# Piece 22 of each expert loaded as 112 and twice 8 partitions

## The chip, the cores and the metric

One core of a Trainium2 chip. The metric is the device time of one execution in microseconds (us), median over runs. A core has five engines (TensorE or PE, VectorE or DVE, ScalarE or ACT, GpSimd or POOL, SyncE or SP) and 16 transfer engines, which move data between the chip's main memory and its on-chip memory of 128 partitions. SP issues nearly all transfers here, in one queue; a transfer of 128 partitions is spread over all 16 transfer engines, eight partition rows each.

## What is computed

A two-layer decoder on 256 tokens of width 1024, in float32: latent attention, a dense feed-forward block, sliding-window attention, and then a mixture of experts, a final norm at the end. The experts are what matters here:

```python
gates = ...                                     # top 2 of 8 experts per token, softmax over the two
hg = jnp.einsum('sd,edf->sef', xs, w_gate)      # e = 8 experts, d = 1024, f = 3584
hu = jnp.einsum('sd,edf->sef', xs, w_up)
hh = jax.nn.silu(hg) * hu * gs[..., None].astype(xs.dtype)
return jnp.einsum('sef,efd->sd', hh, w_down)
```

Each expert has three matrices of 1024 x 3584 float32 values, 44 MB together, and all eight experts are read once: 352 MB.

## The kernel before, in words

The dense part takes the first 400 us. Then come eight items, one per expert (more only if an expert has over 96 tokens). The experts are ordered at run time, so that those with up to 64 tokens ("narrow") and those with more ("wide") come in a fixed pattern; a narrow item is less work for TensorE, while every item has the same weights.

An expert's weights come in 24 pieces of 128 partitions x 3584 values (14336 bytes per partition, 1792 KB): pieces 0 to 7 of the gate matrix, 8 to 15 of the up matrix, 16 to 23 of the down matrix (the list `pieces`, `NP` = 24). A ring of eight places in on-chip memory holds them. SP runs `load_item`: for each piece it waits in `room_for` until TensorE has read what lies in that place, and issues the transfer. Its semaphore is one of eight (`landing`), each raised by 16 for a landed piece. Piece 23 is loaded as two halves by columns (L708 and L709 in the profile), the second on the semaphore `tail_landed`, so that TensorE can begin with its first half.

TensorE takes an item in this order (`pe_item`): the products with the eight gate pieces (`products`, L1569), among them the scatter of the item before (L1587); those with the eight up pieces (L1569); the first 14 rows of the down product (`down`, L1611 and L1612 in a narrow item, L1544 to L1548 in a wide one); the gather of the next item's tokens (L1535); and the other 14 down rows. A down row is 1024 columns wide, so that 3.5 rows lie in a piece: row r begins at column 1024 r of the down pieces, and piece 16 + n at column 3584 n. A row in a narrow item is two passes of a pair of matmuls (L1611 and L1612, side by side). `down` waits for a piece with `piece_here` before the first row that reaches into it: for piece 22 before row 21, for the second half of piece 23 before row 26. The wait is on the whole count, so a piece is there when the last of its transfer engines has finished.

Instructions are themselves brought in by transfers, in the queue named "instruction" (q8), in packets of 16 KB.

Of the kernel before, what the change touches and what calls it, by code (L numbers as in the profile page):

```python
# [37 lines left out]
P = 128  # L38
# [90 lines left out]
class Semaphores:  # L129
    def __init__(self, sem):  # L130
# [124 lines left out]
        self.ahead_loaded_a = sem("ahead_loaded_a")  # L255
        self.ahead_loaded_c = sem("ahead_loaded_c")
        self.tail_landed = sem("tail_landed")
        self.gu_read = sem("gu_read")
        self.gate_mm = sem("gate_mm")
        self.sg_ready = sem("sg_ready")  # L260
# [21 lines left out]
def build(nc, x, positions, w_in, g_q, g_kv, w_uq, w_ukv, w_o, kv_g, kv_w, kv_b, swa_w_q, swa_b_q,  # L282
          swa_sinks, swa_w_o, swa_b_o, rel_bias, g_attn, g_ffn, f_gate, f_up, f_down, w_router,
          e_gate, e_up, e_down, g_final, consts, out):
    with ExitStack() as ctx:
# [12 lines left out]
        s = Semaphores(lambda name: ctx.enter_context(nc.semaphore(name)))  # L298
# [253 lines left out]
        pieces = [(kind, 0, k) for kind in "gu" for k in range(KD)]  # L552
        pieces += [("d", half, part) for half in range(2) for part in range(TILES * D // PIECE)]
        NP = len(pieces)
        DOWN0 = 2 * KD
        assert NP % LAPS == 0 and KD == LAPS
        ppos = {p_: m for m, p_ in enumerate(pieces)}
        whole = ring[:].rearrange("p a n -> p (a n)")

        def turn_of(m, first):  # L560

            return m if first and m < 2 * KD - OUTSIDE else m - OUTSIDE

        def place(m, first):

            return PIECE * ((FIRST_AT + turn_of(m, first)) % LAPS)

        def landing(m, first):

            return s.piece_landed[turn_of(m, first) % LAPS]  # L570
# [5 lines left out]
        def piece_here(eng, i, m, first):  # L576

            if first and m in AHEAD_A:
                eng.wait_ge(s.ahead_loaded_a, 16 * OUTSIDE)
            else:  # L580
                eng.wait_ge(landing(m, first), i * (16 * NP // LAPS) + 16 * (turn_of(m, first) // LAPS + 1))

        def piece(m, first):
            if first and m in AHEAD_A:
                return AHEAD_A[m]
            return whole[:, place(m, first):place(m, first) + PIECE]

        def down_row(r):

            c0 = (place(DOWN0, False) + D * r) % (LAPS * PIECE)  # L590
            return whole[:, c0:c0 + D]

        def down_pieces(r):

            return range(DOWN0 + D * r // PIECE, DOWN0 + (D * r + D - 1) // PIECE + 1)

        def last_down_row(m):

            return (PIECE * (m + 1 - DOWN0) - 1) // D

        def in_tail(r):

            return D * r + D > PIECE * (NP - DOWN0) - PIECE // 2

# [45 lines left out]
        def _(sp):  # L650
# [11 lines left out]
            def piece_of_expert(m, expert):  # L662
                kind, half, part = pieces[m]
                if kind == "d":
                    return ed[:, expert, half, part * PIECE:(part + 1) * PIECE]
                return (eg if kind == "g" else eu)[:, expert, part, :]

            def room_for(i, m, first):

                if m < LAPS:  # L670
                    if not first:
                        sp.wait_ge(s.down_mm, i * (2 * TILES) + (last_down_row(m + 2 * LAPS) + 2 - 2 * TILES))
                        return
                    for sl in dense_under(m):
                        if sl >= 5:
                            sp.wait_ge(*used_up(NU - 1))
                        else:
                            sp.wait_ge(*stream[earlier_fill(DENSE, sl)][4:6])
                    return
                under = m - LAPS  # L680
                if first and m >= DOWN0:
                    in_ring = [p_ for p_ in range(NP) if p_ not in AHEAD_A]
                    under = in_ring[in_ring.index(m) - LAPS]
                kind, _, k = pieces[under]
                if k < KD - 1:
                    sp.wait_ge(s.gu_read, i * (2 * KD - 2) + ((KD - 1) * (kind == "u") + k + 1))
                else:
                    sp.wait_ge(s.gate_mm if kind == "g" else s.up_mm, i * (2 * THIRDS) + 2 * THIRDS)

            def load_item(i, expert, first):  # L690
                for m in range(NP):
                    if first and m == 5:
                        sp.wait_ge(s.spT_mm, AH)
                        for ma, room in AHEAD_A.items():
                            sp.dma_start(room, piece_of_expert(ma, expert)).then_inc(s.ahead_loaded_a, 16)
                    if first and m == LAPS:
                        sp.wait_ge(s.swo_mm, 4)
                        sp.wait_ge(s.router_mm, 2)
                        for ma, room in AHEAD_C.items():
                            sp.dma_start(room, piece_of_expert(ma, expert)).then_inc(s.ahead_loaded_c, 16)  # L700
                    if first and (m in AHEAD_A or m in AHEAD_C):
                        continue
                    room_for(i, m, first)
                    if m < NP - 1:
                        sp.dma_start(piece(m, first), piece_of_expert(m, expert)).then_inc(landing(m, first), 16)
                    else:
                        src, mid = piece_of_expert(m, expert), PIECE // 2
                        sp.dma_start(piece(m, first)[:, 0:mid], src[:, 0:mid]).then_inc(landing(m, first), 16)  # L708
                        sp.dma_start(piece(m, first)[:, mid:PIECE], src[:, mid:PIECE]).then_inc(s.tail_landed, 16)  # L709

            load_item(0, 0, True)
            sp.wait_ge(s.counts_ready, 1)
            sp.wait_ge(s.order_ready, 1)
            with sp.Fori(1, NE) as i:
                load_item(i, sp.value_load(order[0:1, bass.ds(i, 1)], min_val=0, max_val=NE - 1), False)

            items = sp.value_load(n_items[0:1, 0:1], min_val=NE, max_val=ITEMS_MAX)
            for sweep in range(1, SWEEPS):
                with sp.If(items > sweep * NE):
                    with sp.Fori(0, NE) as e:  # L720
                        load_item(e + sweep * NE, sp.value_load(order[0:1, bass.ds(e, 1)], min_val=0, max_val=NE - 1), False)
                with sp.Else():
                    sp.nop()
# [356 lines left out]
        def _(pe):  # L1080
# [460 lines left out]
            def wide_step(bank, slots, left, right, first, last):  # L1541
                thirds = [slots[:, 32 * j:32 * j + 32] for j in range(3)]
                for j in range(3):
                    pe.matmul(ps[32 * j:32 * j + 32, bank, :], thirds[j], left, start=first, stop=last)  # L1544
                pe.matmul(ps[SLOTS:P, bank, :], thirds[2], right, start=first, stop=last)  # L1545
                for j, cols in ((0, 0), (1, 0), (0, LASTQ), (1, LASTQ)):
                    q = 32 * j + cols // 4
                    mm = pe.matmul(ps[q:q + 32, bank + 1, 0:LASTQ], thirds[j], right[:, cols:cols + LASTQ], start=first, stop=last)  # L1548
                return mm
# [46 lines left out]
            def down(i, half, j, narrow, first_item):  # L1596
                r = half * TILES + j
                for m in down_pieces(r):
                    if r == 0 or m not in down_pieces(r - 1):
                        piece_here(pe, i, m, first_item)  # L1600
                if in_tail(r) and not in_tail(r - 1):
                    pe.wait_ge(s.tail_landed, i * 16 + 16)
                if r == 0:
                    pe.wait_ge(s.sgt_ready, i + 2)
                if j == 0:
                    pe.wait_ge(s.hhT_ready, i * 2 + (half + 1))
                w = down_row(r)
                first, last = r == 0, r == 2 * TILES - 1
                if narrow:
                    lhs = hhT[:, half, j, 0:NARROW]  # L1610
                    pe.matmul(ps[0:NARROW, DOWN_BANK, :], lhs, w[:, 0:512], start=first, stop=last)  # L1611
                    mm = pe.matmul(ps[64:64 + NARROW, DOWN_BANK + 1, :], lhs, w[:, 512:1024], start=first, stop=last)  # L1612
                else:
                    mm = wide_step(DOWN_BANK, hhT[:, half, j, :], w[:, 0:512], w[:, 512:1024], first, last)
                mm.then_inc(s.down_mm, 1)
# [555 lines left out]
```

## Time and profile before

| | |
|---|---|
| median of 3 runs | 1222.96 us (1222.02 to 1223.16) |
| profiled execution, its own time | 1221.85 us |
| its span, first to last instruction | 1220.0 us |
| mean granted TensorE clock | 0.989 of full speed |
| TensorE matmul busy | 1163.6 us, 95% of the span |
| moved by transfers | 413.44 MB, 339 GB/s over the span |
| expert phase | from about 403 to 1208 us |

TensorE's busy share and the transfer engines' share are both near full in the expert phase. A share of 1.00 of the transfer engines means that all 16 are at work; it can read a little above 1, as packets of one engine overlap slightly. Items of the expert phase are numbered 0 to 7.

### The profile page before, as it was taken

How to read it: one execution, taken by the hardware profiler on the slowest of the kernel's cores; microseconds unless marked ns; L12 is line 12 of the kernel's file. 1: busy time of each engine (PE TensorE's matmuls, PEld its weight loads, DVE VectorE, ACT ScalarE, POOL GpSimd, SP SyncE). 2: the span in 40 equal slices, each digit the busy share in tenths (PEclk: the TensorE clock that was granted, in tenths of full speed). 3: DMA queues.
4: the chain of work that ended last, by engine and by line, in shares of the span. 5: the costliest groups of instructions: out<-in, count | busy, mean ns of one | idle time of the engine just before them, and what ended most of it. 6: DMA issues, size and time to landing. Idle time of an engine off the chain costs nothing.

```text
span 1220.0 us, 21797 instructions
## 1 busy us (share of the span) xinstructions
PE 1163.6 (95%) x9461; PEld 584.5 (48%) x9462; DVE 338.9 (28%) x727; ACT 212.9 (17%) x399; POOL 40.0 (3%) x69
## 2 busy tenths in 40 slices
PE   7999999999999999799899999999989989998997
PEld 5878777778765534233233433333343333333323
DVE  3666566666372302002002010110201101020112
ACT  2454333333263100000010000001010010101001
POOL 2130000000200010000000000000000000000000
PEclk9999999999999999899899999999999999999999
DMA  9614645237534999999999999999999999999994
GB/s 338 243 69 161 229 162 190 87 138 256 220 122 181 375 417 426 415 427 425 425 425 426 414 414 426 425 426 425 426 426 425 426 425 426 425 424 424 421 425 195
DMA packets 56044, 413.44 MB, mean 339 GB/s; under 512 B 4702, under 2 KB 10076, under 8 KB 32140
## 3 DMA queue, kind: packets, MB, share of 16 engines
q1 hardware_dynamic: 54464, 410.40, 82.1%
q8 instruction: 82, 1.34, 0.4%
q0 software_dynamic: 944, 1.29, 0.3%
q10 hardware_dynamic: 540, 0.29, 0.1%
q14 instruction: 14, 0.11, 0.0%
HBM read 410.91 MB, written 1.05 MB: 338 GB/s over the span
## 4 chain that ended last, share of the span: by engine, by line
PE 85%; DMA 4%; DVE 4%; issue 4%; ACT 2%; ACTq 0%; POOL 0%; POOLq 0%; DVEq 0%; SPq 0%
PE ps L1569 36%; PE ps L1611 7%; PE ps L1544 6%; PE ps L1256 4%; PE ps L1252 4%; PE ps L1253 4%; PE ps L1548 3%; PE ps L1587 3%; PE ps L1535 2%; PE ps L1428 2%; DMA ring<-in_moe_w_gate 2%; DMA ring<-in_moe_w_down 2%; PE ps L1379 2%; PE ps L1115 2%; ACT w_hi L912 1%
## 5 line engine op out<-in xcount | busy, mean ns | idle before, releaser
L1569 PE MATMUL ps<-ring,arena 128*32 128x448 f32 x4800 | 465.9, 547 | 23.9 <-issue 21.7
L1569 PEld LDWEIGHTS ps<-ring,arena 128*32 128x32 f32 x4800 | 155.6, 111 | 327.0 <-issue 324.5
L1611 PE MATMUL ps<-ring,arena 128*64 128x512 f32 x280 | 122.9, 594 | 8.2 <-DVE arena L2111 5.1
L1612 PE MATMUL ps<-ring,arena 128*64 128x512 f32 x280 | 122.9, 594 | 0.0
L2106 DVE TENSOR_TENSOR arena<-arena,ps 128x448 f32<-128x448 f32 x38 | 22.3, 605 | 285.1 <-PE ps L1569 284.7
L1544 PE MATMUL ps<-ring,arena 128*32 128x512 f32 x504 | 87.0, 593 | 2.4 <-DVE arena L2111 2.4
L1852 DVE TENSOR_TENSOR w_lo<-ring,w_hi 128x2048 fp32r<-128x2048 f32 x31 | 71.1, 2292 | 57.1 <-ACT w_hi L912 55.1
L1545 PE MATMUL ps<-ring,arena 128*32 128x512 f32 x168 | 85.9, 593 | 0.0
L1611 PEld LDWEIGHTS ps<-ring,arena 128*64 128x64 f32 x280 | 37.2, 137 | 87.1 <-issue 71.6
L912 ACT CAST w_hi<-ring 128x2048 fp32r<-128x2048 f32 x31 | 59.1, 1909 | 112.9 <-PE ps L1256 112.9
L2088 DVE TENSOR_TENSOR h<-h,ps 128x512 f32<-128x512 f32 x36 | 24.8, 688 | 186.3 <-PE ps L1587 186.3
L1024 ACT ACTIVATE arena<-ps 128x448 f32<-128x448 f32 x38 | 20.6, 543 | 258.0 <-PE ps L1569 257.2
L1252 PE MATMUL ps<-w_hi,xT_hi 128*128 128x512 f32 (+1 forms) x176 | 64.9, 376 | 0.0
L1253 PE MATMUL ps<-w_hi,xT_lo 128*128 128x512 f32 (+1 forms) x176 | 63.9, 370 | 0.0
L1031 ACT ACTIVATE arena<-ps,vecT 128x96 f32<-128x96 f32 x36 | 9.3, 341 | 299.5 <-PE ps L1535 299.5
L1548 PE MATMUL ps<-ring,arena 128*32 128x256 f32 x672 | 51.6, 379 | 0.0
L1548 PEld LDWEIGHTS ps<-ring,arena 128*32 128x32 f32 x672 | 21.8, 110 | 50.3 <-issue 50.3
L1256 PE MATMUL ps<-w_lo,xT_hi 128*128 128x512 f32 (+1 forms) x176 | 41.4, 379 | 0.0
L1612 PEld LDWEIGHTS ps<-ring,arena 128*64 128x64 f32 x280 | 37.2, 137 | 0.0
L1587 PE MATMUL ps<-arena 96*128 96x512 f32 x72 | 35.6, 618 | 0.8 <-ACT arena L1055 0.8
L1252 PE MATMUL ps<-w_hi,fhhT_hi 128*128 128x512 f32 x88 | 34.8, 395 | 1.4 <-DVE h L1921 1.4
L1535 PEld LDWEIGHTS ps<-arena,xn 128*128 128x128 f32 x288 | 32.9, 192 | 6.2 <-issue 5.9
(306 smaller groups left out, 1157.9 us busy)
## 6 DMA issues: line engine op xcount, KB each, us to landing
ring<-in_moe_w_gate SPq DMA_DIRECT2D x64, 1792.0 KB, 19.2
ring<-in_moe_w_up SPq DMA_DIRECT2D x61, 1792.0 KB, 16.5
ring<-in_moe_w_down SPq DMA_DIRECT2D x56, 1792.0 KB, 21.1
ring<-in_moe_w_down SPq DMA_DIRECT2D x16, 896.0 KB, 22.0
ring<-in_ffn_w_gate SPq DMA_DIRECT2D x5, 2048.0 KB, 7.8
ring<-in_ffn_w_up SPq DMA_DIRECT2D x5, 2048.0 KB, 7.8
ring<-in_ffn_w_down SPq DMA_DIRECT2D x5, 2048.0 KB, 7.9
ring<-in_mla_w_o SPq DMA_DIRECT2D x2, 2048.0 KB, 24.6
```

The costliest lines, as they stand in the source:

```text
L912: act.copy(hi, w).then_inc(s.whi_ready, 1)
L1252: pe.matmul(out, lhs[0][:, k, c], rhs_hi[:, k, :], start=(first and k == 0), stop=False)
L1253: pe.matmul(out, lhs[1][:, k, c], rhs_hi[:, k, :], start=False, stop=False)
L1256: mm = pe.matmul(out, lhs[0][:, k, c], rhs_lo[:, k, :], start=False, stop=(last and k == nk - 1))
L1544: pe.matmul(ps[32 * j:32 * j + 32, bank, :], thirds[j], left, start=first, stop=last)
L1545: pe.matmul(ps[SLOTS:P, bank, :], thirds[2], right, start=first, stop=last)
L1548: mm = pe.matmul(ps[q:q + 32, bank + 1, 0:LASTQ], thirds[j], right[:, cols:cols + LASTQ], start=first, stop=last)
L1569: mm = pe.matmul(ps[Q * q:Q * q + Q, bank_of(a, j), 0:CH], lhs, w[:, c0:c0 + CH], start=first, stop=last)
L1587: pe.matmul(ps[:, SCATTER_BANK[j], :], sgt[0:SLOTS, t, :], ysb[0:SLOTS, half * 512:(half + 1) * 512], start=True, stop=True).then_inc(s.sc ...
L1611: pe.matmul(ps[0:NARROW, DOWN_BANK, :], lhs, w[:, 0:512], start=first, stop=last)
L1612: mm = pe.matmul(ps[64:64 + NARROW, DOWN_BANK + 1, :], lhs, w[:, 512:1024], start=first, stop=last)
L1852: dve.tensor_tensor(lo, w, hi.bitcast(F32), ALU.subtract).then_inc(s.wlo_ready, 1)
```

## The change

Piece 22 (`CORNERED = NP - 2`) of each expert is no longer one transfer of 128 partitions. SP issues two of eight partitions, 112 to 119 and 120 to 127, on a semaphore of their own, and then one of partitions 0 to 111 on the piece's usual semaphore. The large one is spread over all 16 transfer engines as seven rows each; each of the small ones goes as one row to each of eight engines, so that eight engines get nine rows of the piece, and eight get seven. The bytes and their places are the same. TensorE waits for the new semaphore too, right after the piece's own, before row 21. SP waits for room as before, once, ahead of the three.

```diff
+        self.corner_landed = sem("corner_landed")
...
+        CORNERED, CORNERS = NP - 2, ((P - 16, P - 8), (P - 8, P))
...
                     room_for(i, m, first)
-                    if m < NP - 1:
+                    if m == CORNERED:
+                        room, src = piece(m, first), piece_of_expert(m, expert)
+                        for p0, p1 in CORNERS:
+                            sp.dma_start(room[p0:p1, :], src[p0:p1, :]).then_inc(s.corner_landed, 16)
+                        whole_rows = CORNERS[0][0]
+                        sp.dma_start(room[0:whole_rows, :], src[0:whole_rows, :]).then_inc(landing(m, first), 16)
+                    elif m < NP - 1:
                         sp.dma_start(piece(m, first), piece_of_expert(m, expert)).then_inc(landing(m, first), 16)
...
                         piece_here(pe, i, m, first_item)
+                        if m == CORNERED:
+                            pe.wait_ge(s.corner_landed, i * (16 * len(CORNERS)) + 16 * len(CORNERS))
```

## Rows read from the trace of the kernel before

**Rows 1.** The page: share and rate of the transfer engines in 40 equal slices.
```profile
DMA  9614645237534999999999999999999999999994
GB/s 338 243 69 161 229 162 190 87 138 256 220 122 181 375 417 426 415 427 425 425 425 426 414 414 426 425 426 425 426 426 425 426 425 426 425 424 424 421 425 195
```

**Rows 2.** Stretches of 100 us: busy times, then clock, transfer share, GB/s.
```profile
800.00:900.00 100.00, 99.22 (x1057) 37.44 (x1053) 12.64 (x21) 4.66 (x11) 0.00 (x0) 1.00 1.01 425
900.00:1000.00 100.00, 93.02 (x794) 33.57 (x786) 11.45 (x20) 6.98 (x15) 0.00 (x0) 0.98 1.01 425
```

**Rows 3.** TensorE's waits, 499 to 1200 us: total, times, longest (us).
```profile
PE ps L1569 <- issue: 21.7, 5, 9.1
...
PE ps L1611 <- DMA ring<-in_moe_w_down: 3.0, 2, 1.5
...
PE ps L1569 <- DMA ring<-in_moe_w_gate: 2.1, 1, 2.1
```

**Rows 4.** Transfers in the chain that ended last: start, length (us).
```profile
972.95 27.81 DMA ring<-in_moe_w_gate
...
1165.00 23.44 DMA ring<-in_moe_w_down
```

**Rows 5.** SP's timeline: issue of the gate pieces of items 6 and 7.
```profile
972.95 26.41 SPq L705 DMA_DIRECT2D ring<-in_moe_w_gate  x8
...
1084.42 35.05 SPq L705 DMA_DIRECT2D ring<-in_moe_w_gate  x8
```

**Rows 6.** TensorE's timeline in the down rows of item 7: start, length (us).
```profile
1177.83 0.64 PE L1611 MATMUL ps<-ring,arena 128*64 128x512 f32 x1 [1.00 <-DVE arena L2111]
...
1183.46 0.59 PE L1611 MATMUL ps<-ring,arena 128*64 128x512 f32 x1
...
1184.14 0.64 PE L1611 MATMUL ps<-ring,arena 128*64 128x512 f32 x1
...
1186.34 0.59 PE L1611 MATMUL ps<-ring,arena 128*64 128x512 f32 x1
...
1188.48 0.64 PE L1611 MATMUL ps<-ring,arena 128*64 128x512 f32 x1 [1.54 <-DMA ring<-in_moe_w_down]
...
1195.81 0.64 PE L1611 MATMUL ps<-ring,arena 128*64 128x512 f32 x1
```

**Rows 7.** End of the weight stream: stretch, length, clock, transfer share, GB/s.
```profile
1194.00:1196.00 2.00, 1.00 1.03 434
...
1198.00:1199.00 1.00, 1.00 0.51 203
...
1202.00:1203.00 1.00, 1.00 0.52 215
...
1205.00:1206.00 1.00, 1.00 0.00 0
```

**Rows 8.** Queues from 794 to 898.6 us: packets, MB, share of 16 engines.
```profile
q1 hardware_dynamic: 3622, 44.37, 100.2%
q8 instruction: 9, 0.15, 0.6%
```

**Rows 9.** The same columns as in rows 7, 695 to 696 us.
```profile
695.00:696.00 1.00, 1.00 0.64 272
```

**Rows 10.** TensorE's timeline at the start of item 6.
```profile
1000.99 1.33 PE L1569 MATMUL ps<-ring,arena 128*32 128x448 f32 x12 [2.14 <-DMA ring<-in_moe_w_gate]
```

**Rows 11.** SP's timeline: issue of the two halves of piece 23, item 7.
```profile
1177.02 0.33 SPq L708 DMA_DIRECT2D ring<-in_moe_w_down  x1
1177.54 0.33 SPq L709 DMA_DIRECT2D ring<-in_moe_w_down  x1
```

**Rows 12.** The lines L708 and then L709: their eight issues to landing.
```profile
DMA to landing us min/median/max: 13.3/20.9/26.4
...
DMA to landing us min/median/max: 15.0/22.5/28.0
```

**Rows 13.** Transfers to few partitions: times, KB each, us to landing.
```profile
posk_i<-in_positions POOLq DMA_DIRECT2D x4, 8.0 KB, 5.4
```

## Prediction

> **What bounds the kernel now.** I read the page's slices first, then the stretches, TensorE's waits, the chain of waits, the timelines, and last the end of the weight stream and the queues. The reader is to see three things.
>
> First, in the expert phase two resources are nearly full at once. From the page's slices the transfer engines (DMA engines) are full from about 430 us to almost the end [rows 1], and in a stretch of 100 us they show a share of 1.01 at 425 GB/s while TensorE is busy for 99.22 us; in another it is busy for only 93.02 us at the same transfer rate [rows 2]. So the weights come at one steady pace, and TensorE is sometimes ahead of them and sometimes not.
>
> Second, where TensorE really waits for a transfer. After 499 us its waits are 21.7 us without a releaser, in five places at the start of an item, 2.1 us for a gate piece, 3.0 us for down pieces [rows 3]. The chain of waits goes through two transfers: one from 972.95 to 1000.76 us and one from 1165.00 to 1188.44 us [rows 4]. The first is gate piece 0 of item 6, the last but one of eight: SP issued that item's gate pieces from 972.95 us, those of item 7 from 1084.42 [rows 5]. The second is found by counting down rows: a row is two pairs of matmuls 0.43 us apart, row 0 begins at 1177.83, and the gap of 1186.34 to 1188.48 lies before row 10 [rows 6]. Row 10 is the first that reaches into piece 19 (columns from 10752). Between these two landings lie 24 + 19 = 43 pieces in 1188.4 - 1000.8 = 187.6 us: 4.36 us for one, 104.7 us for the 24 of an item. From 1000 us the pace of the weights sets the end; before, TensorE mostly does.
>
> Third, whose pace that is. A piece is 128 rows of 14336 bytes, eight for each of 16 engines; at 425/16 = 26.6 GB/s a row takes 0.54 us. But the engines do not finish together: at the end of the stream the share falls from 1.03 to 0.51 at 1198 us, stays near 0.5 until 1203 and is zero from 1205 [rows 7]. With nothing left to issue, a share of one half means that eight engines have finished and eight have about 6.5 us to go. A landing counts only when the last engine is done, so the late eight set the pace, and the early eight lead them. The instruction queue shows where such a lag can come from: nine packets of 16 KB in the stretch of one item, which go to single engines and not to all [rows 8]. The lead is also trimmed on the way: at 695 us the share falls to 0.64 for a microsecond, since the early ones had nothing queued [rows 9]. Eight packets per item and eight late engines fit: 6.5 us over the last five to seven items is 0.9 to 1.3 us per item, more than 16384 bytes at 26.6 GB/s (0.6 us), but of that size.
>
> **The change part by part.** Removed: one transfer of 128 rows per item. Added: one of 112 rows, seven per engine, and two of eight rows, one row on each of eight engines. Those eight get nine rows of piece 22, the other eight get seven; bytes are the same. All eight items do it.
>
> Engine time, if a row costs what it costs now: +0.54 us per item on eight engines, -0.54 us on the other eight. If the seven go to the late eight, the landing of piece 0 of item 6 comes 6 x 0.54 = 3.2 us sooner, that of piece 19 in item 7, before that item's own piece 22, 7 x 0.54 = 3.8 us, and the tail of item 7 4.3 us sooner. The engines with nine must not become the last. At the end they had about 6.5 us in hand; relative to the others they lose 7 x 1.08 = 7.6 us by piece 19. Taken alone this puts them 1.1 us behind and the gain at 2.7 us. But they also ran dry at 695 [rows 9] and, being later now, would not: that gives back one or two microseconds. So 2.7 to 3.8 us; I take 3.7, since at a share of 0.64 each early engine loses 0.36 x 16/8 = 0.7 us in that microsecond alone, and pays the start of a new transfer besides.
>
> What TensorE can take of it: the wait of 2.14 us at item 6 [rows 10], and 0.25 us at 1184.14 and 1.71 us at 1188.48, each a start-to-start time less the usual 0.43 [rows 6]: together 4.1 us, besides 1.5 us for a down piece before 1000 us [rows 3]. The smaller of 4.1 and 3.7 counts: 3.7 us. The profiled execution took 1221.85 us (span 1220.0 and 1.85 around it), 1.1 less than the median of the runs; the sum gives 1218.15 for it, and 1219.3 for the median. The tail does not undo it. It lands at 1177.5 + 28.0 = 1205.5 us [rows 11, 12]; row 26 of the down product, which needs it, begins near 1206.2 (row 14 at 1195.81 [rows 6], then 0.86 us a row), and it moves with the others. Further ahead little is to be had: of TensorE's waits after 499 us only three ended with a transfer, those 1.5 us, the 2.14 and the 1.54 [rows 3].
>
> Issue: SP issues two more transfers per item. One is 0.33 us, and the next follows 0.52 us later [rows 11], so some 1.0 us per item. Queued behind them are the rest of piece 22, the two halves of piece 23, and the next item's pieces. They land typically 20.9 to 22.5 us after issue [rows 12], so the engines have some four pieces queued; the delay is hidden as long as that holds. If the queue were empty it would cost 1.0 us per item. The shortest landing of the first half of piece 23 is 13.3 us [rows 12], still three pieces. TensorE gets one more wait per item, before row 21; its weight load sits idle about 0.3 us before each pass, and a passed wait is taken as nothing (upper bound 8 x 0.1 us).
>
> What the trace does not show is the price of a row in the two small transfers. Eight rows go at the same time into eight neighbouring partitions, 112 to 119 and then 120 to 127, while other engines write their own. Lower bound: 0.54 us a row, as now. Upper bound: the eight share what one engine moves now, 8 x 0.54 = 4.3 us for each transfer, 7.5 us more per item than at the lower bound. The nearest rows are loads of 32 and fewer partitions of 8 KB and less, 5.4 us to landing [rows 13], which excludes neither. I take the lower bound, because every row of the stream so far runs at 26.6 GB/s whatever the phase of the other engines, but both ends stay for the range.
>
> The Trainium skill speaks against this part. "SBUF — State Buffer", section "Door 1: The DMA port swizzle", says that a transfer's rate depends on how many of 16 ports its partitions reach, four neighbouring partitions (and those 32 above) sharing one; a 16-partition load was measured there at 104 GB/s. By that page 112 to 119 are two ports, and the estimate from it is 2.1 us for each small transfer instead of 0.54. This trace has no large transfer on few partitions, so no run here shows it.
>
> "DMA: Bandwidth & Descriptors", section "Why a DMA increments its semaphore by 16 and not by 1", says that a transfer of eight partitions from SP uses the lowest-numbered eight engines. The trace carries no engine numbers, so it does not say whether these are the early ones.
>
> **The rivals.**
> (a) Forecast: the early eight get nine, rows keep their price. 1222.96 - 3.7 = 1219.3 us.
> (b) The rows of the small transfers slow each other. Place: piece 22 of each item, on the engines with nine. Price: four rows in turn instead of side by side, 2 x (4 x 0.54 - 0.54) = 3.2 us per item. The engines with nine now need about 104.7 - 1.2 + 0.5 + 3.2 = 107.2 us per item against 104.7: 2.5 us x 8 = 20 us later, 1243 us (at the upper bound, 7.5 us per item, some 40 to 50 us more than now); more than 1243 if the engines that write these partitions anyway are held up as well. It decides from 0.5 us per item on: there it eats the whole gain, and above it the kernel is slower. For it: all these rows are issued at once into neighbouring partitions. Against: the early eight's lead, and no such slowing in this trace. The page on SBUF above is this rule.
> (c) The late eight get nine. Nothing in the trace names them. +0.54 x 7 = 3.8 us at piece 19: 1226.8 us.
> (d) No effect that can be measured: a small extra price of 0.2 to 0.5 us per item, or the late group differs from one execution to the next, so that the two halves cancel. 1222 us.
>
> **How the numbers follow.** (a) 0.47, (b) 0.30, (c) 0.10, (d) 0.13. A difference of 0.2% (2.45 us) is about what can be told from no change. Of (a) I give 0.04 to a gain below that; of (b) 0.02 to a price so small that it is in the band. Faster 0.44, same 0.18, slower 0.38. The prediction is (a), 1219.3 us, in its own range 1218.6 to 1221 us. The range over the cases goes up to 1244 us, the value of (b) just inside, and leaves out the worse part of (b), where both groups are held up or the upper bound holds: 0.13 above it, 0.02 below.
>
> **What would show it.** In the profile after: the fall of the share at the end of the stream should go from 1.0 to 0 within some 2 us instead of 6.5; the gate wait of 2.14 us at item 6 should be gone and that before row 10 smaller; the stream's end should come near 1201 us. Under (b) the rate over a stretch of 100 us drops below 420 GB/s, TensorE waits for transfers in most items, and the small transfers take longer to land than their neighbours. Under (c) the half-share stretch at the end grows to 10 us or more. The prediction is wrong if the small rows cost over 1 us each, if the late engines are those with nine, or if SP's extra issues meet an empty queue.

## The result, and the profile after

The median of four runs is 1316.3 us (1313.33 to 1319.92) against 1222.81 us of four runs before: a ratio of 1.0761, 95% interval 1.0746 to 1.0776. The change makes the kernel 93.5 us slower. The profiled execution took 1318.39 us, its span is 1316.6 us.

The page first: the rate and share of the transfer engines in 40 slices, then the queue of the weights and the issues of the down pieces (times, KB each, median us to landing).

```profile
DMA  9516444348258999999999999999999999999991
GB/s 343 200 61 255 162 160 160 129 163 309 77 203 352 412 348 424 427 336 424 427 363 356 426 427 263 427 426 350 314 423 427 278 384 410 404 310 411 426 308 60
...
q1 hardware_dynamic: 54592, 410.40, 82.3%
...
ring<-in_moe_w_down SPq DMA_DIRECT2D x48, 1792.0 KB, 27.6
```

Beside [rows 1] the second line says nearly all. The share is full in the same part of the span, but the rate is no longer one flat 425: it falls to 260 to 360 GB/s once or twice per item and comes back to 427 between. So the engines are not short of work there; what they do takes longer, and only for a while.

TensorE's waits from 480 to 1310 us (total, times, longest); L1621 and L1577 are the lines L1611 and L1569 of before, L1552 is L1544.

```profile
PE ps L1621 <- DMA ring<-in_moe_w_down: 51.0, 23, 6.1
PE ps L1577 <- issue: 24.7, 5, 9.1
PE ps L1577 <- DMA ring<-in_moe_w_up: 18.1, 18, 1.2
PE ps L1552 <- DMA ring<-in_moe_w_down: 4.9, 2, 4.5
```

The three rows with a transfer stand for 43 waits and 74 us; the three such waits of before were worth 5.1 us [rows 3]. The waits without a releaser have hardly moved (24.7 us, 21.7 before). Up pieces make TensorE wait too, so the delay is not over with piece 22.

The same in stretches of 100 us, 500 to 1300 (columns as in rows 7 of before):

```profile
500.00:600.00 100.00, 0.94 1.01 396
600.00:700.00 100.00, 0.98 1.01 386
700.00:800.00 100.00, 0.98 1.01 411
800.00:900.00 100.00, 0.95 1.01 384
900.00:1000.00 100.00, 0.97 1.01 363
1000.00:1100.00 100.00, 0.93 1.00 363
1100.00:1200.00 100.00, 0.99 1.00 376
1200.00:1300.00 100.00, 0.96 0.83 321
```

Together they moved 300 MB in 800 us. At 425 GB/s that takes 706 us: 94 us less, about the whole loss.

Where in an item it lies: SP's timeline at piece 22 of item 2, and the stretches behind it.

```profile
675.51 0.81 SPq L709 DMA_DIRECT2D ring<-in_moe_w_down  x2
676.49 0.32 SPq L711 DMA_DIRECT2D ring<-in_moe_w_down  x1
```

```profile
680.00:684.00 4.00, 1.00 1.13 326
684.00:688.00 4.00, 1.00 0.96 186
688.00:692.00 4.00, 1.00 1.01 219
692.00:696.00 4.00, 1.00 0.93 177
696.00:700.00 4.00, 1.00 1.02 233
700.00:704.00 4.00, 1.00 1.03 336
704.00:708.00 4.00, 1.00 1.01 427
```

From 684 to 700 us all 16 engines are busy and move 204 GB/s, half of the usual. That is 3.3 MB, nearly two pieces, where the changed piece alone has 1.8 MB. Pieces next to it are drawn in. The trace's records of single rows say it too. In these 16 us every row of 14336 bytes took 0.74 to 1.38 us, where the usual one takes 0.54, and there are 164 of them, more than the 128 of piece 22. Every half row of piece 23 took 0.36 to 0.77 us, where 0.27 is usual.

TensorE has 1189.8 us of matmul time against 1163.6, with a mean granted clock of 0.973 against 0.989: some matmuls behind a wait run at a lower clock. That this costs nothing is a reading, not a measurement: the transfer engines are full all the while, and the weights' pace sets the time.

### The profile page after: what moved, and what is told of

Read it like the earlier page. It is cut to its first block, busy times and chain, and to the rows that moved or that the text cites. A ratio compares the mean times of both kernels' runs of the same rounds, so it can differ in the third digit from the quotient of the medians.

```text
span 1316.6 us, 21849 instructions
## 1 busy us (share of the span) xinstructions
PE 1189.8 (90%) x9461; PEld 587.1 (45%) x9462; DVE 338.8 (26%) x727; ACT 213.0 (16%) x399; POOL 40.0 (3%) x69
## 4 chain that ended last, share of the span: by engine, by line
PE 65%; DMA 26%; issue 3%; DVE 3%; ACT 2%; ACTq 0%; SPq 0%; POOL 0%; POOLq 0%; DVEq 0%
PE ps L1577 27%; DMA ring<-in_moe_w_down 12%; DMA ring<-in_moe_w_gate 9%; DMA ring<-in_moe_w_up 4%; PE ps L1552 4%; PE ps L1264 4%; PE ps L1260 4%; PE ps L1261 4%; PE ps L1621 2%; PE ps L1595 2%; PE ps L1436 2%; PE ps L1556 2%; PE ps L1387 2%; PE ps L1123 2%; PE ps L1543 1%
## 5 line engine op out<-in xcount | busy, mean ns | idle before, releaser
L1577 PE MATMUL ps<-ring,arena 128*32 128x448 f32 x4800 | 471.1, 549 | 44.2 <-issue 24.7
L1577 PEld LDWEIGHTS ps<-ring,arena 128*32 128x32 f32 x4800 | 155.2, 111 | 353.2 <-issue 317.5
L1621 PE MATMUL ps<-ring,arena 128*64 128x512 f32 x280 | 140.3, 652 | 53.2 <-DMA ring<-in_moe_w_down 51.0
L1622 PE MATMUL ps<-ring,arena 128*64 128x512 f32 x280 | 140.4, 652 | 0.0
L1621 PEld LDWEIGHTS ps<-ring,arena 128*64 128x64 f32 x280 | 39.0, 149 | 147.8 <-issue 88.1
L1552 PE MATMUL ps<-ring,arena 128*32 128x512 f32 x504 | 88.5, 601 | 7.3 <-DMA ring<-in_moe_w_down 4.9
L1553 PE MATMUL ps<-ring,arena 128*32 128x512 f32 x168 | 87.3, 602 | 0.0
L2098 DVE TENSOR_TENSOR h<-h,ps 128x512 f32<-128x512 f32 x36 | 24.7, 687 | 189.7 <-PE ps L1595 189.7
L2132 DVE TENSOR_TENSOR arena<-ps,vecT 128x384 f32<-128x384 f32 x8 | 4.5, 557 | 140.0 <-PE ps L1543 140.0
L1622 PEld LDWEIGHTS ps<-ring,arena 128*64 128x64 f32 x280 | 39.0, 149 | 0.0
```

Of the source, the lines that this page charges most:

```text
L1577: mm = pe.matmul(ps[Q * q:Q * q + Q, bank_of(a, j), 0:CH], lhs, w[:, c0:c0 + CH], start=first, stop=last)
```

## The experiments

Three theories. A: any partition range other than all 128 makes several transfer engines write at once through the same entrance (the way into memory that a few partitions share, the prediction's port), the large 112-row transfer as much as the small ones. B: only the two small transfers do so, and the 112 rows keep their price. C: the number of transfers, issues and waits costs.

### First four: the parts of the change alone

Each stands in place of the three transfers of the change (`room` is the place in the ring, `src` the piece). One run of each and one of before (1222.27 us), on one chip; four runs of the change spread over 6.6 us, so differences of a few us between these are not to be read. The cuts of the code show the transfers alone. TensorE waits for `corner_landed` as in the change, but not in "112 alone", which never raises it.

**112 and 16.** The two small transfers made one.

```diff
+    sp.dma_start(room[112:128, :], src[112:128, :]).then_inc(s.corner_landed, 16)
+    sp.dma_start(room[0:112, :], src[0:112, :]).then_inc(landing(m, first), 16)
```

> Piece 22 of each item as one transfer of 16 partitions (112 to 127) and one of 112; every engine has eight rows, and no transfer of eight partitions is left. Theory A (the 112-partition transfer spreads its rows so that engines meet at the same partitions' entrance, and all of them slow down): most of the 93 us stay, 1290 to 1340 us. Theory B (the two transfers of eight partitions are what costs): nearly all of it goes, below 1245 us. Theory C (the nine rows on the wrong eight engines, or SP's extra issues): 1223 to 1227 us.

Measured: 1304.06 us, +81.8. So of the 93.5 us some 12 go with having two small transfers instead of one of 16 rows.

**112 alone.** Rows 112 to 127 of piece 22 are not loaded at all.

```diff
+    sp.dma_start(room[0:112, :], src[0:112, :]).then_inc(landing(m, first), 16)
```

> Only partitions 0 to 111 of piece 22 are loaded (rows 112 to 127 of it keep what an earlier piece left there, so the output is another one); seven rows per engine. Theory A: still 50 us or more above 1223. Theory B and theory C: 1216 to 1222 us, since there is less to load.

Measured: 1298.97 us, +76.7, with less to load. In the stretches behind item 2's piece 22:

```profile
684.00:688.00 4.00, 1.00 0.93 189
688.00:692.00 4.00, 1.00 1.05 224
692.00:696.00 4.00, 1.00 0.96 211
696.00:700.00 4.00, 1.00 0.98 397
```

The half rate is there with no small transfer in the kernel, only for 12 us instead of 16. This excludes B as the main cause: the 112-row transfer does it alone. (With rows left out the output is another one; the time is what counts here.)

**64 and 64.**

```diff
+    sp.dma_start(room[0:64, :], src[0:64, :]).then_inc(s.corner_landed, 16)
+    sp.dma_start(room[64:128, :], src[64:128, :]).then_inc(landing(m, first), 16)
```

> Piece 22 as two transfers of 64 partitions; four rows of each per engine. Theory A: a half of the partitions is a half of the entrances, so each row costs up to twice: 4 us or more per item, 1250 to 1300 us. Theory B and theory C: within 3 us of 1223.

Measured: 1329.32 us, +107.1, more than the change. From 900 to 1000 us the weights' queue (packets, MB, share of 16 engines) shows, of this kernel:

```profile
q1 hardware_dynamic: 2980, 35.98, 100.2%
```

and of before in the same stretch:

```profile
q1 hardware_dynamic: 3473, 42.41, 100.2%
```

The engines are as full and move 15% less.

**The small ones alone.** Partitions 112 to 119 and 120 to 127 are loaded as in the change; rows 0 to 111 of piece 22 are not loaded.

```diff
+    sp.dma_start(room[112:120, :], src[112:120, :]).then_inc(s.corner_landed, 16)
+    sp.dma_start(room[120:128, :], src[120:128, :]).then_inc(landing(m, first), 16)
```

> Only partitions 112 to 127 of piece 22 are loaded, as the two transfers of eight (the other 112 rows are left out, so the output is another one). Theory A in its strict form (the 112 rows are the cause): below 1223 us. Theory B: the 93 us stay less the 3.7 us per item of the rows left out: 1280 us or more. If rows in a small transfer cost up to four times a usual one, 3.2 us per item more on eight engines, the two nearly cancel: 1215 to 1225 us.

Measured: 1223.31 us, +1.0. The time alone says little here, since leaving out 112 rows saves 3.8 us of transfer per item, of which TensorE could have taken only some 4 us in all. The rate says more (500 to 1100 us):

```profile
500.00:600.00 100.00, 0.98 1.01 412
600.00:700.00 100.00, 1.00 1.01 412
700.00:800.00 100.00, 0.98 1.00 404
800.00:900.00 100.00, 1.00 1.01 415
900.00:1000.00 100.00, 0.98 1.01 414
1000.00:1100.00 100.00, 1.00 1.01 415
```

412 GB/s on average with full engines: 3% short of 425, about 3 us per item. The prediction gave rival (b) 3.2 us of lost time on eight engines and 2.5 us in the pace of an item. The pace is near that, but here the 3 us are a mean over all sixteen engines, twice (b)'s engine time. The records of single rows show whose it is. After 430 us, 496 rows of 14336 bytes took over 0.7 us, 127 in the kernel before; the small transfers have only 128 rows in all. So rows of the full pieces are slowed too. Half rows of piece 23 over 0.38 us are 442 of 2048, 5 before.

### Theory C: two transfers of all 128 partitions

**Halves by columns.**

```diff
+    sp.dma_start(room[:, 0:mid], src[:, 0:mid]).then_inc(s.corner_landed, 16)
+    sp.dma_start(room[:, mid:PIECE], src[:, mid:PIECE]).then_inc(landing(m, first), 16)
```

> Piece 22 as two transfers of all 128 partitions, half the columns each, with a semaphore and a wait of its own, as in the change. Theory A (partition ranges other than the full 128 are the cause): no change, within 2 us of 1223. Theory C (one more transfer, wait or issue by SP costs): over 1225 us.

Measured: 1223.63 us (10 runs) against 1223.24 (16 runs), ratio 1.000, 0.999 to 1.001. One more transfer, issue, semaphore and wait per item cost nothing that can be measured. C is out as a cause of this size.

### The same extra rows, in other partitions

Before, plus three extra loads per item in items 1 to 7 (with pieces 4, 12 and 20), of eight partitions by 8192 bytes, into space that nothing reads; TensorE waits for each together with its piece. The bytes and the count are equal; the partitions differ: every fourth of 0 to 28, every fourth of 64 to 92, or 112 to 119. The rows of the piece that are read differ with them, since each load takes the rows of its own partitions.

```diff
+    if not first and m in (4, 12, 20):
+        sp.dma_start(early_row[0:29:4, 0:2048], piece_of_expert(m, expert)[0:29:4, 0:2048]).then_inc(s.extra_landed, 16)
```

**0, 4, ..., 28.**

> The kernel before, with three extra loads of eight partitions x 8192 bytes in each of items 1 to 7 (24.6 KB per engine, 0.9 us at the usual rate, to unused space): partitions 0, 4, ..., 28. If the eight engines that a transfer of eight partitions uses are the early ones, and each meets nobody at its partition: within 1.5 us of 1223. If they are the late ones: 0.9 x 7 = 6 us more, 1229 us.

**64, 68, ..., 92.**

> The same three extra loads into partitions 64, 68, ..., 92, which in a load of 128 partitions other engines write. If two engines then meet at each entrance, the late ones lose up to what is loaded extra, 0.9 us per item: 1226 to 1232 us, between the spread and the adjacent one. If only neighbours in one transfer matter: as the spread one.

**112 to 119.**

> The same three extra loads into partitions 112 to 119, all next to each other. If four neighbouring partitions share an entrance, a row takes four times as long: 3.7 us per item on eight engines, 2.4 beyond the lead that they gain, and the engines that write there anyway are held up too: 1235 to 1255 us. If neighbours don't matter: as the spread one.

Measured: 1227.91 us (ratio 1.0034, 1.0022 to 1.0046), 1239.54 us (1.0127, 1.0110 to 1.0144) and 1250.18 us (1.0214, 1.0197 to 1.0231): +4.7, +16.3 and +26.9 us. What the eight engines have more to do is 3 x 8192 bytes per item, 0.92 us at 26.6 GB/s, 6.5 us over seven items. The first costs less than that. The other two cost 12 and 22 us on top, for as many bytes in as many rows. So which partitions a transfer covers sets the price. That it is the writing into them and not the reading of their rows is not separated here; the rule below speaks for the writing. Nor is it mainly the extra rows that take longer. By the trace's records of single rows, their medians are 0.31, 0.32 and 0.32 us in the three runs, and 0.31 us is usual for 8192 bytes. But of the rows of 14336 bytes, which belong to the full pieces, 148, 514 and 700 took over 0.7 us (after 430 us). The weights' queue from 900 to 1000 us, of the first of these kernels:

```profile
q1 hardware_dynamic: 3497, 42.37, 100.1%
```

of the second:

```profile
q1 hardware_dynamic: 3383, 41.78, 100.3%
```

of the third:

```profile
q1 hardware_dynamic: 3345, 41.48, 100.0%
```

The Trainium skill, "SBUF — State Buffer", section "Door 1: The DMA port swizzle", gives the rule: partitions 0, 4, ..., 28 and 64, 68, ..., 92 are eight different entrances each, 112 to 119 two. "DMA: Bandwidth & Descriptors", section "The descriptor swizzle", adds whose they are: in a transfer of 128 partitions, partitions 0 to 63 are written by the lower eight engines and 64 to 127 by the upper eight, each to one entrance. If the eight rows go to the eight lower engines in order, these write at their own entrances in the first run, at those of the other eight in the second, and crowd two of the others' in the third. The order of the three times agrees. Which row goes to which engine no trace here shows.

### Is 96 and 32 better, and who are the late ones?

**96 and 32.** In the form of the first experiments, with partitions 96 to 127 and then 0 to 95.

> Piece 22 of each expert is loaded as 32 partitions (96 to 127) and 96 partitions (0 to 95). Theory A (any range of partitions other than the full 128 makes engines meet at the same partitions, so that their rows take twice as long and pieces behind are drawn in): much slower, 1290 to 1340 us, like 112 and 16 (1304) and 64 and 64 (1329). Theory B (only small transfers on neighbouring partitions cost): 32 partitions are four times the 8 of one corner, so the loss per row would be smaller: below 1240 us. If 96, a multiple of 16 and of 32, is spread without meetings, the time is near 1225 us, and theory A would hold for 112 and 64 alone.

Measured: 1320.13 us (one run), against 1223.51 before on its chip. The loss that A foresees is there for each of the splits 64, 96 and 112.

The run with extra rows in 0, 4, ..., 28 told one more thing, at the end of the stream:

```profile
1206.00:1207.00 1.00, 1.00 0.53 208
1207.00:1208.00 1.00, 1.00 0.50 208
1208.00:1209.00 1.00, 1.00 0.31 129
1209.00:1210.00 1.00, 1.00 0.14 57
1210.00:1211.00 1.00, 1.00 0.12 50
1211.00:1212.00 1.00, 1.00 0.12 50
```

A share of 0.12 is two of 16. Two engines now end last, some 3 us behind the next ones. This looked as if the late eight of before were two of the eight with extra rows and six of the other half. To find the two, the same loads with fewer partitions:

**0, 4, 8, 12.**

> Before plus, in items 1 to 7, three extra loads of 4 partitions by 8192 bytes (partitions 0, 4, 8, 12, written to space that nothing reads), so that only the four lowest-numbered engines have more to do, 0.92 us per item each. If the two engines that ended last in the run with eight of them (+4.7 us) are among these four, the loss stays at 4 to 5 us and two of 16 engines are the last at the end of the stream (share 0.12); if none is, no measurable change, 1223 us, and the share at the end stays at one half until 5 us after the first fall. If one is, the loss is the same and the share at the very end is 0.06.

**0, 4, ..., 20.**

> As the run with four partitions, with six (partitions 0, 4, 8, 12, 16, 20), so that the six lowest-numbered engines have 0.92 us more per item. If the two last engines are numbers 4 and 5, this is 4 to 5 us slower than before and the run with four is not; if they are 6 and 7, neither is; if they are among the first four, both are.

Measured against 1223.51 us: 1222.57 us (ratio 0.9989, 0.9980 to 0.9999) with four, so no loss; 1227.28 us (1.0026, 1.0016 to 1.0036) with six. The difference between them is the rows in 16 and 20. The end of the stream with six:

```profile
1205.00:1206.00 1.00, 1.00 0.36 151
1206.00:1207.00 1.00, 1.00 0.12 50
1207.00:1208.00 1.00, 1.00 0.07 29
```

First two engines, then one. If a transfer of four or six partitions goes to the four or six lowest-numbered engines, as the Trainium skill's "DMA: Bandwidth & Descriptors", section "Why a DMA increments its semaphore by 16 and not by 1", has it, the two that get more to do only in the second are numbers 4 and 5 (counted from 0). What is shown is that the rows in 16 and 20 cost 4 us where those in 0 to 12 cost nothing. That they go to these two engines rests on the Trainium skill, and that one or both of them are late is the reading that fits.

## Why the prediction was wrong

It forecast 1219.3 us, a gain of 3.7, in a range up to 1244. The loss is 93.5 us.

**The step that failed** is the first sentence of the sum: "Engine time, if a row costs what it costs now: +0.54 us per item on eight engines, -0.54 us on the other eight." The doubt was put on the rows of the two small transfers only. The 112-row transfer was counted as seven rows per engine at the usual price without a question, though no row of the trace showed a large transfer of other than 128 partitions. It costs 76.7 us when it stands alone, over four fifths of the loss. The stretch from 684 to 700 us runs at 204 GB/s with all engines busy: the rows there take about twice as long, those of piece 22 and those of its neighbours. After 430 us, 2153 of 21663 rows of 14336 bytes took over 0.7 us, against 127 of 21646 before.

**The price of the small rows** was taken at the lower bound, "because every row of the stream so far runs at 26.6 GB/s whatever the phase of the other engines". But nearly every such row was part of a transfer of 128 partitions, in which, if A is right, each engine keeps to its own entrance; the argument held only for those. With the 112 rows left out, the two small transfers slow the stream by about 3 us per item, near the 2.5 of rival (b)'s pace and six times its deciding point of 0.5. So (b) was right in the direction and in the pace of its own part. It was not right in whose rows are slowed: it priced only those of the small transfers, on eight engines, and most of the slowed rows belong to full pieces. Its 1243 us also left out the large transfer. The sentence "more than 1243 if the engines that write these partitions anyway are held up as well" points the right way, but it was left out of the range. (A slip beside it, without weight: by its own parts the chance of faster is 0.47 - 0.04 = 0.43 and that of same 0.19, not 0.44 and 0.18.)

**The late eight.** "If the seven go to the late eight" supposed that they are one half by number. The runs with extra rows speak against it: by the numbering of the Trainium skill cited above, rows on the four lowest engines cost nothing, so these are not late; with rows on two more the loss is 4 us, so the late ones are not simply the upper eight; and when eight have more to do, two engines end last. Had no rows met, and had the small transfers gone to the same eight engines as the extra rows, the change would, with two late engines among these eight, have taken 0.54 us per item from six late engines and added as much to the two others, which set the landing. Then (c), not (a), would have come out, at most 8 x 0.54 = 4.3 us slower. This is argued: no run shows the change without its collisions.

**Right, though not enough.** The weights' pace sets the end: 94 us of lost transfer account for 93.5 us of time. One more issue and one more wait are free: the split by columns shows 1.000. Of the signs named, two of (b) came: a rate below 420 GB/s in each 100 us (363 to 411, and 321 in the last, which has the end of the stream in it), and 46 waits for transfers in eight items. The third can't be read, since the profile gives no landing of the small transfers. The signs of the forecast did not come; at the end the share, instead of going to zero within 2 us, tails off over 20:

```profile
1275.00:1280.00 5.00, 0.78 0.91 321
1280.00:1285.00 5.00, 1.00 0.23 75
1285.00:1290.00 5.00, 1.00 0.19 63
1290.00:1295.00 5.00, 1.00 0.17 68
1295.00:1300.00 5.00, 1.00 0.07 29
1300.00:1304.00 4.00, 1.00 0.03 13
```

Some four engines of 16 are behind the others here, then three, then one. A landing counts only when the last is done, so this is paid as well. Before it was half of them by 6.5 us [rows 7].

**What stays open.** Shown is that one large transfer of fewer than 128 partitions per item does it, and that for small ones it depends on which partitions. Not shown is the meeting at the entrances itself. No run keeps the partitions written and changes the rows read, or the other way round. Why a slow stretch lasts 16 us or more after one changed piece is argued too: an engine with a row of piece 22 still to write at another's entrance meets that engine when it is already at the next piece, and slows both. No run varied the distance to the pieces behind. Nor does a run show where 112 rows are placed on the 16 engines. Where the lag of the late engines comes from is open as well; a 16 KB packet of instructions took 1.07 us (median of 62 after 430 us, before), which is in the prediction's 0.9 to 1.3 us per item, but nothing ties these packets to the late engines.

No better version came out. To relieve the late engines, others must load partitions that are not theirs, and the runs with rows in 64 to 92 and 112 to 119 suggest what that costs.

## What to carry to other kernels

Keep each large transfer at all 128 partitions when the transfer engines are the bound, and cut it by columns if it must be cut: this cost nothing, while 64, 96 or 112 partitions once in 24 pieces cost 6 to 9% of the kernel. When a price is taken from a trace, ask which rows it was seen on: a rate that holds for many equal transfers says nothing of the first one of another shape. And before work is balanced between two groups of engines, find out who is in them; a share of one half tells how many are late, not which.

## What the runs showed of the hardware

- One 112-partition transfer per item halves the rate of all 16 engines for 12 us or more (189 to 224 GB/s at a share of about 1.0). Twice 64 partitions is the worst of the splits (+107.1 us); 96 and 32 (+96.6) and 112, 8 and 8 (+93.5) can't be told apart, one being a single run; 112 and 16 cost +81.8. The rule on the number of entrances in the Trainium skill, "SBUF — State Buffer", section "Door 1: The DMA port swizzle", doesn't foresee this: by it 112 and 96 partitions reach all sixteen. So that number is not enough; that each engine has to be at its own is the reading that fits.
- The rows that take longer are not only those of the odd transfer: with 112, 8 and 8, all rows from 684 to 700 us took longer than usual, those of pieces 22 and 23 and others.
- Eight rows of 8192 bytes cost 0.2, 0.8 or 1.3 us of the kernel each time (4.7, 16.3 and 26.9 us for 21), according to the partitions (and the rows read with them). The rows that became slower are mostly those of the full pieces.
- Extra rows in partitions 0 to 12 cost nothing, with 16 and 20 added +3.8 us. So the transfer engines are not equally far behind; by the Trainium skill's numbering, cited above, one or both of the fifth and sixth are among the late.
